# Two mixing stages whose engines each follow a planned order of small parts, with the merge's gates made inside them and kept in memory

## The reference, cut to what matters

```python
h = rms_norm_2(x, norm_mix[l])
z = h @ w_in[l]
c_q, c_kv, k_pe, hq, hf, hi, hg, g_a, g_b = jnp.split(z, offsets, axis=-1)
y_a = mla_mixer(c_q, c_kv, k_pe, ...) @ w_proj_a[l]
y_b = hgrn2_mixer(hq, hf, hi, hg, lower_bounds[l], ...) @ w_proj_b[l]
y = jax.nn.sigmoid(g_a) * y_a + jax.nn.sigmoid(g_b) * y_b
x = x + y @ w_out[l]
h = rms_norm_2(x, norm_ffn[l])
x = x + (jax.nn.silu(h @ w_gate[l]) * (h @ w_up[l])) @ w_down[l]
```

## Time and profile before

| | |
|---|---|
| median of 3 runs | 4867.03 us (4865.81 to 4867.9) |
| the profiled execution | 4877.7 us, of which the span of the page is 4876.4 |
| first block and what leads to layer 0's mixing | 2496.4 us |
| mixing stage, layer 0 / layer 1 | 616.7 / 616.3 us |
| merge and output product, layer 0 / layer 1 | 174.9 / 174.8 us |

### The profile page before, as it was taken

One profiled execution on the slowest core, in us unless ns is written; L12 is line 12 of the kernel. 1 busy time (PEld: TensorE's weight loads), 2 busy tenths in 40 slices (PEclk: granted clock), 3 DMA queues, 4 the chain that ended last, 5 costly groups with the idle time before them and its releaser, 6 DMA issues.

```text
span 4876.4 us, 51844 instructions
## 1 busy us (share of the span) xinstructions
PE 3921.2 (80%) x20620; PEld 3270.0 (67%) x20620; DVE 1520.6 (31%) x2463; ACT 1426.5 (29%) x2119; POOL 1356.5 (28%) x778
## 2 busy tenths in 40 slices
PE   7778888878889859999956555799998655588999
PEld 6767777777777757777655434587887543467887
DVE  2445455455440221111132533221102253313110
ACT  1322333433432200000033433333323433333331
POOL 1323334333324311101031211243442111134443
PEclk9888889989889958889977656899998766689999
DMA  4222201110103248879720100132332100022332
GB/s 135 70 57 57 57 27 31 31 27 22 31 22 104 59 117 277 270 248 291 252 80 26 31 9 13 35 100 81 96 95 55 39 21 2 13 57 82 92 98 87
DMA packets 467349, 401.74 MB, mean 82 GB/s; under 512 B 17910, under 2 KB 427043, under 8 KB 466981
## 3 DMA queue, kind: packets, MB, share of 16 engines
q1 hardware_dynamic: 456117, 361.70, 25.0%
q0 software_dynamic: 9520, 30.97, 1.9%
q10 hardware_dynamic: 1472, 5.77, 0.3%
HBM read 381.86 MB, written 16.53 MB: 82 GB/s over the span
## 4 chain that ended last, share of the span: by engine, by line
PE 71%; DVE 12%; ACT 9%; POOL 4%; issue 2%; DMA 1%; SPq 0%; DVEq 0%; ACTq 0%; POOLq 0%
PE bank L233 30%; PE bank L237 12%; PE bank L239 12%; PE bank L238 12%; ACT AR L134 5%; DVE AR L107 5%; POOL AR L107 3%; ACT L134 3%; DVE AR L118 2%; DVE AR L112 2%; PE bank L243 2%; PE bank L900 1%; DVE AR L126 1%; PE bank L1879 1%; POOL HTl L107 0%
## 5 line engine op out<-in xcount | busy, mean ns | idle before, releaser
L233 PE MATMUL bank<-AR 128*128 128x128 f32 (+5 forms) x5712 | 983.3, 332 | 412.8 <-POOL AR L107 247.5
L107 POOL TENSOR_TENSOR ring_r<-ring,high_r 128x1024 fp32r<-128x1024 f32 (+1 forms) x345 | 820.9, 2379 | 1424.4 <-ACT high_r L134 1416.4
L233 PEld LDWEIGHTS bank<-AR 128*128 128x128 f32 (+3 forms) x5712 | 847.2, 226 | 531.3 <-issue 270.7
L134 ACT ACTIVATE AR<-bank 128x512 f32<-128x512 f32 (+6 forms) x803 | 398.4, 496 | 1990.8 <-PE bank L233 1053.8
L107 DVE TENSOR_TENSOR AR<-AR,bank 128x512 f32<-128x512 f32 (+1 forms) x411 | 263.8, 642 | 1458.2 <-PE bank L239 766.9
L237 PE MATMUL bank<-HTh,high_r 128*128 128x512 f32 (+1 forms) x1608 | 658.7, 410 | 29.7 <-DVE HTl L107 13.3
L238 PE MATMUL bank<-HTl,high_r 128*128 128x512 f32 (+1 forms) x1608 | 640.6, 398 | 0.0
L239 PE MATMUL bank<-HTh,ring_r 128*128 128x512 f32 (+1 forms) x1608 | 640.1, 398 | 0.0
L134 ACT ACTIVATE high_r<-ring 128x1024 fp32r<-128x1024 f32 (+1 forms) x345 | 363.7, 1054 | 262.6 <-DMA ring<-in_w_down 141.9
L107 POOL TENSOR_TENSOR AR<-AR 128x512 f32<-128x512 f32 x112 | 167.0, 1491 | 822.2 <-ACT AR L134 817.7
L237 PEld LDWEIGHTS bank<-HTh,high_r 128*128 128x128 f32 (+1 forms) x1608 | 312.8, 195 | 97.3 <-DVE HTl L107 13.8
(11 more groups left out here) (146 smaller groups left out, 4877.6 us busy)
## 6 DMA issues: line engine op xcount, KB each, us to landing
ring<-in_w_in SPq DMA_DIRECT2D x154, 512.0 KB, 4.1
ring<-in_expert_w SPq DMA_DIRECT2D x61, 1024.0 KB, 11.2
high<-in_expert_w SPq DMA_DIRECT2D x60, 1024.0 KB, 11.8
ring<-in_ada_w SPq DMA_DIRECT2D x48, 512.0 KB, 4.0
ring<-in_w_gate SPq DMA_DIRECT2D x44, 512.0 KB, 3.8
ring<-in_w_up SPq DMA_DIRECT2D x44, 512.0 KB, 3.8
ring<-in_w_down SPq DMA_DIRECT2D x44, 512.0 KB, 3.6
AR<-in_expert_w SPq DMA_DIRECT2D x20, 1024.0 KB, 12.0
```

Source lines behind the costliest of these rows:

```text
L107: self.did(self.e.tensor_tensor(out, a, b, op), inc)
L134: self.did(self.e.activation(out, a, func, **kw), inc)
L233: m = pe.matmul(outap, l, r, start=(i == 0), stop=(i == n - 1))
```

## The change

The two hand-written lists, their interleaving and the banks of each are gone. In their place the stage is described as parts: each has one engine, a time in us by hand, the parts that it needs, and the bank that it opens or closes. A dense product of eight steps is eight parts.

`plan` simulates the five engines with these numbers. Each free engine takes, of its ready parts, the one with the longest way still behind it. Only PE has a second source: when none of its small parts is ready, it takes the next step of the dense products, which stand in one list in a fixed order. All eight banks are shared. What comes out is an order of its own for each engine, which `pe_mix`, `act_mix`, `vec_mix` and `pool_mix` then issue. The plan is made when the program is built; on the chip every queue is still in order.

```diff
+    HOP = 0.3
+    def plan(parts, fifo, nbank, spare, keep):
...
+            far[k] = parts[k][1] + HOP + max((far[n] for n in then[k]), default=0.0)
...
+                k = max((k for k in ready[e] if fits(k, keep.get(k[0], 0))), key=lambda k: far[k], default=None)
+                if k is not None:
+                    ready[e].remove(k)
+                elif e == "P" and head < len(fifo) and not left[fifo[head]] and fits(fifo[head], spare):
+                    k, head = fifo[head], head + 1
...
+    def mix_parts():
...
+            if what[-1] != "R":
+                part(("hi", i), "A", 1.05, ("load", i), *([("hi", hi[0])] if hi[0] is not None else []))
+                part(("lo", i), "G", 2.45, ("hi", i), *([("lo", hi[0])] if hi[0] is not None else []))
...
+        def gates(ns):
+            for i in ns:
+                dense(("G", i), 8, 0.69, [tile_of("in", 0, 1024, 2720 + i * 128, 128, "G")], opens=("G", i))
+                part(("Ga", i), "A", 1.7, ("G", i, 7), *([("Gs", i - 2)] if i > 1 else []))
+                part(("Gv", i), "V", 0.7, ("Ga", i), closes=("G", i))
+                part(("Gx", i), "A", 0.8, ("Gv", i))
+                part(("Gs", i), "S", 5.0, ("Gx", i))
...
+                for n in range(NT):
+                    part(("rn", wi, n), "V" if wi == 0 else "G", (1.9, 4.4)[wi], ("qi", wi))
+                    part(("rp", wi, n), "V" if wi == 0 else "G", (1.8, 3.0)[wi], ("rn", wi, n))
...
+        latent("cq", 0, 384, 384)
+        projection("f", 0)
+        latent("ck", 384, 256, 288)
+        projection("q", 0)
+        values(0)
+        projection("g", 0)
+        attention_in()
+        for h in range(1, 4):
+            projection("f", h)
+            projection("q", h)
+            if h == 2:
+                values(h)
+            projection("g", h)
+            gates(range(4 * h - 4, 4 * h))
+        gates(range(12, 16))
+        attention()
+        recurrence()
```

```diff
+            elif x in ("ga", "f1", "Ga"):
...
+                A.act(dst, mix_bk(g, i)[:, :], ACT.Abs)
+                A.act(dst, dst, ACT.Exp, scale=-1.0)
+                A.act(dst, dst, ACT.Ln, bias=1.0, inc=aEv)
+            elif x == "Gx":
...
+                A.act(stg[i % 2], stg[i % 2], ACT.Exp, inc=aEv)
+                see(A, "Gx", i)
+                gst[i % 2].then_inc(ac.dma_start(gate_d(i), stg[i % 2]), 16)
...
-            elif k == "g":
-                A.act(ybT[:, p[0]], b[:, :], ACT.Silu, inc=aEv)
```

```diff
+    def act_branch(l, its, MTp):
+        for q in range(2):
+            gst[q].upto(A, gst[q].n)
+        for j in range(16):
+            if j < 4:
+                act_gate(j)
...
+            act_split(it["t"] + HEAD)
+            if j + 4 < 16:
...
+                act_gate(j + 4)
...
+    def act_gate(i):
+        gld[i % 4].then_inc(ac.dma_start(tn2[:, i % 4], gate_d(i)), 16)
...
         sp_load(mg[0]["t"] - 1)
+        act_split(t0 + 1)
         act_squares(xn2, x_ready)
         act_norm(NT, 0, HT, tmpm)
-        act_split(its[0]["t"] + 2)
         vec_rows(xn2)
         vec_norm(NT, 0, HT, tmpm, lambda k: cb(f"mix{l}", k), None)
+        pool_split(t0 + 1)
         pool_norm(NT, 0, HT, tmpm)
-        pool_split(its[0]["t"] + 2)
```

More of the change, by code:

```diff
@@ new lines, in build, with mix_tiles @@
+    pt, fifo, mix_spec = mix_parts()
+    mix_order, mix_bank, mix_before, mix_last, mix_when = plan(pt, fifo, 8, 3, {"QK": 2, "Q": 2})
+    mix_at, mix_n = {}, {}
+    for e, o in mix_order.items():
+        mix_n[e] = 0
+        for k in o:
+            if k in mix_tile and (*k[:-1], k[-1] + 1) in mix_tile:
+                continue
+            if k[0] not in ("load", "hi", "lo", "Gs"):
+                mix_at[k[:-1] if k in mix_tile else k] = (e, mix_n[e])
+                mix_n[e] += 1
+    def mix_tiles(l):
+        src = {"in": d["w_in_2"][l], "uq": d["mla_w_uq_2"][l], "ukv": d["mla_w_ukv_2"][l]}
+        L_ = {"t0": len(tiles), "P": count["group"], "A": count["act"], "V": count["vec"], "old": dict(user)}
+        end = {}
+        for k in mix_order["P"]:
+            if k in mix_tile:
+                end[mix_tile[k]] = max(end.get(mix_tile[k], 0), mix_at[k[:-1]][1])
+        for i, (w, r0, r1, c0, n, how) in enumerate(mix_spec):
+            t = tile(src[w][r0:r1, c0:c0 + n], (r1 - r0) // 128, n, how)
+            tiles[t]["free"] = count["group"] + end[i] + 1
+        for e, n in (("P", "group"), ("A", "act"), ("V", "vec")):
+            count[n] += mix_n[e]
+        for b in range(8):
+            e, i = mix_at[mix_last[b]]
+            user[b] = {"ev": "act" if e == "A" else "vec", "e": L_[e] + i}
+        return L_
@@ new lines, in build, with see @@
+    gEv = sig("mix_part_pool")
+    gst = [sig(f"gate_stored{i}") for i in range(2)]
+    gld = [sig(f"gate_load{i}") for i in range(4)]
+    stg = [flat(cm[:, 2 + 4 * i:6 + 4 * i, :]) for i in range(2)]
+    gate_d = lambda i: y_d[i * 64:(i + 1) * 64, :].rearrange("r (a n) -> (r a) n", n=SEQ)
+    Lc = [None]
+    def see(q, *k):
+        e, i = mix_at[k]
+        if e == "G":
+            gEv.wait_ge(q, i + 1)
+        else:
+            {"P": pD, "A": aEv, "V": vEv}[e].upto(q, Lc[0][e] + i + 1)
@@ new lines, in pe_mix @@
+                    see(P, "le", h, 6)
+                    for j in range(NT):
+                        see(P, "va", h - h % 2, j)
+                see(P, "cv", h, n - 1) if n else see(P, "cz", h)
+                pD.then_inc(mm(tl(mix_bk("out", h), n), [(Sh, tl(qe, n)), (vtoken(h, n), AT[:, n])]))
+            elif x == "cu":
+                h, n = p
+                mix_free(*k)
+                see(P, "Tka", h)
+                for j in range(NT):
+                    see(P, "va", h - h % 2, j)
+                pD.then_inc(mm(mix_bk(*k)[:, 0:128], [(kdt[:, n], vtoken(h, n))]))
+            elif x == "op":
+                mix_free(*k)
+                see(P, "oa", p[0])
+                pD.then_inc(mm(mix_bk(*k)[:, :], [(ones, f1)]))
@@ L2402, in pe_ffn @@
     def pe_ffn(its):
         for it in its:
-            pe_proj(it)
+            w = pe_weight(it["t"])
+            bank_free(P, it)
+            for q in range(8):
+                m = mm3(bk[it["b"]][:, :], w[:, q, :], HT[:, q, :], q == 0, q == 7)
+            pD.then_inc(m)
     def act_ffn(its, end):
@@ L2430, in layer @@
         L_ = layers[l]
-        (its, at), mg, ow, ff, dn = L_["mix"], L_["merge"], L_["out"], L_["ffn"], L_["down"]
+        mg, ow, ff, dn = L_["merge"], L_["out"], L_["ffn"], L_["down"]
+        Lc[0] = L_["mix"]
+        t0 = Lc[0]["t0"]
         end = dn[-1]["t"] if l else last_tile_of_all
@@ L2445, in layer @@
         nV.wait_ge(P, 8)
-        pe_mix(its, at)
-        act_mix(its, at, end)
-        vec_mix(its, at, l)
-        pool_mix(its, at, end)
+        pe_mix()
+        act_mix(l)
+        vec_mix(l)
+        pool_mix(l)
         stage()
```

987 lines of the change are left out of this document (554 added, 433 removed).

## The result

The changed kernel takes 4426.8 us (median of 4 runs, 4407.5 to 4433.5) against 4866.4 before (4 runs): a ratio of 0.910, with an interval from 0.906 to 0.914. Predicted were 4320, with a range from 4220 to 4460. The profiled executions took 4433.5 and 4877.7.

A forecast was written before the change was run, and what follows sets the result against it. Hand-overs between engines bound the mixing stage, PE alone the merge. Per layer, 191.5 us saved in the stage and 81.4 in merge and joint, twice, plus 3.1 at layer 0's start: 548.9 saved, so 4320 us, range 4220 to 4460.

The forecast's parts named there:

- likeliest case: Whole kernel: mixing stage of 425 us, time 4320 us, own range 4240 to 4420, chance 0.70.
- rival 1: Mixing stage: in-order queues keep the hand-over's toll, late parts hold all behind; stage 500, time 4468 us, chance 0.15.
- signs of being wrong: Attention nearer 90 or 150 than 120 us, PE waiting over 20 in A or B, or for VectorE held by GpSimd.
- B: Mixing stage from first turned head of q to first logits: three engines near full together, 60 us.
- A: Mixing stage up to the first turned head of q: 138 us, including 3 for PE's slow clock at start.
- C: Attention stretch of the mixing stage, with head 2 between: 120 us, bounds 88 and 150.
- D: Mixing stage behind the attention, eleven gates and head 3: ScalarE, not PE, sets the end, 107 us.
- The joint: Between mixing stage and merge: PE waits for high and low parts of the attention output, 6 us lost.
- Merge: Merge with output product: the 16 gate products go, 87.4 us remain of 174.9, gate loads covered.
- Rival 2: ScalarE in the mixing stage: every table load costs double; stage 477, time 4422 us, chance 0.02.
- Rivals 3 and 4: Mixing stage: 3, plan holds, stage 370, 4208 us, chance 0.10; 4, waits stay, gates on top, 704, 4876, 0.03.
- rival 5: Merge: the gates' way through memory fails to hide; 5 us a layer, up to 20; no chance of its own.

The follow-up runs named there:

- one table: Changed kernel, but ScalarE loads one table set holding both Exp and Ln and keeps it; layers 536.3 and 533.7 us, against 576.9 and 573.8.
- experiment 3: Changed kernel, replanned with the planner tracking the held table and adding 1.28 us per load; stage 454.6 and 452.2 us, layers 564.2 and 561.2.

## Why the prediction was right, and which of its terms were not

**The sign and the kind** were right: PE's waits for scaled q, 123.8 us before, are 18.4 in the same view of the changed kernel's stage, and its transposes' wait for the probabilities, 83.3, is 7.5:

```profile
PE bank L243 <- DVE AR L107: 21.9, 4, 12.5
...
PE bank L233 <- POOL AR L107: 18.4, 9, 3.7
...
PE bank L243 <- DVE AR L112: 7.5, 7, 2.8
```

**The size** was too good by 58.5 us in layer 0 and 55.4 in layer 1, and the time by 107. It lies beyond the likeliest case's own range, 4240 to 4420, between it and rival 1 (a stage of 500, 4468). It is inside the range over all cases, but two of the prediction's own signs of being wrong came: the stage is over 450, and PE waits in B for more than 20 us (28.2). Nothing in the prediction separated what the order and the gates bring; the order, with what came along with it, brings all of it.

**B, 94 for 60: the step that failed.** "Three engines are near full together: 60" took the means of before and no latency. Two things showed. The table loads are 14 of the 34. For the other 20 the longest piece is head 1's chain: PE waits 12.5 us (11.3 with one table) for VectorE's pair of products, in the view above the longest part of "PE bank L243 <- DVE AR L107", 21.9. In this chain VectorE is slow beside GpSimd. Here are four scans before the change with GpSimd idle (head 0), then those of head 1 in the changed kernel's B, with a weight split that starts 0.41 us behind them, and the products that PE waits for, with k's norm on GpSimd beside them:

```profile
2561.30 1.80 DVE L2346 TENSOR_TENSOR_SCAN AR<-cm,AR 128x128 f32<-128x128 f32 x4
```

```profile
2645.22 3.94 DVE L2539 TENSOR_TENSOR_SCAN AR<-cm,AR 128x128 f32<-128x128 f32 x4
...
2651.25 4.13 DVE L107 TENSOR_TENSOR AR<-AR 128x512 f32<-128x512 f32 x3 [0.90 <-ACT AR L134]
```

```profile
2645.63 2.34 POOL L107 TENSOR_TENSOR ring_r<-ring,high_r 128x1024 fp32r<-128x1024 f32 x1 [5.82 <-ACT high_r L134]
2650.43 3.67 POOL L107 TENSOR_TENSOR AR<-AR 128x768 f32<-128x768 f32 x2 [2.46 <-DVE AR L122]
```

```profile
2654.79 1.09 PE L243 MATMUL bank<-cm,AR 128*128 128x128 f32 x4 [12.53 <-DVE AR L107]
```

The scans lost 3.94 - 1.80 = 2.14 us to a split of 2.34, and the three products about 2.1 (each takes 0.69 by itself). (The Trainium skill, "GPSIMD Engine Reference", Specifications, says that GpSimd and VectorE get in each other's way where VectorE reads two inputs from SBUF, as a scan here does; this trace agrees.) That is some 4 of the 12.5 us; in the rest the chain goes back and forth between ScalarE and VectorE. The prediction saw this, gave it 5 us each in A and C, and none in B. The mean over the stage is 0.96 us for 0.42 before a scan, and 0.89 for 0.75 a product of 512 columns. Measured prices in the plan took back 8 us of the stage. How the 20 us of B divide between VectorE's slowness and plain latency stays open: no run takes GpSimd's weight splits away from VectorE.

**A, 147 for 138.** My 3 us for the clock at the start were in place; the second fall, at the narrow matmuls, was missed. Wide ones give 8.4 and 8.2 us back.

**C, 115 for 120, and D, 112 for 107** were near, in part by luck. C was a choice between bounds, leaning on windows with a clock of 0.65 to 0.83; it ran at 0.90. In D the mechanism was only half right: ScalarE is busy 88.1 of 112.3, 78% and not over 90%, since it waited for PE until gate 11 and is behind PE only from gate 12 on. PE, with 94.3 for the 85 of the sum, is the busier of the two.

**The joint, 16 for 6.** The sum began at PE's last gate step and forgot that gate's own chain. Timelines of the changed kernel: ScalarE from gate 15 on, VectorE's low parts, PE's first branch product.

```profile
2958.86 0.60 ACT L134 ACTIVATE cm<-bank 128x512 f32<-128x512 f32 x1 [0.46 <-ACT cm L134]
...
2962.14 1.28 ACT L134 ACT_TABLE_LOAD   x1
2963.43 0.63 ACT L134 ACTIVATE cm<-cm 128x512 f32<-128x512 f32 x1
...
2964.47 3.35 ACT L134 ACTIVATE high_r<-ring 128x1024 fp32r<-128x1024 f32 x3 [0.40 <-ACT cm L134]
2967.85 5.26 ACT L134 ACTIVATE AR_r<-AR 128x512 fp32r<-128x512 f32 x8
```

```profile
2968.51 8.62 DVE L107 TENSOR_TENSOR AR_r<-AR,AR_r 128x512 fp32r<-128x512 f32 x4 [5.72 <-ACT AR_r L134]
```

```profile
2971.14 0.77 PE L237 MATMUL bank<-AR_r,high_r 128*128 128x512 f32 x1 [16.03 <-DVE AR_r L107]
```

PE stopped at 2955.1, ScalarE finished the gate at 2964.1: 9 us that I hadn't counted. Then 3.4 for the weights, and VectorE's first low part takes 2.2 us beside GpSimd, not 0.69. A gate comes every 5.7 us on ScalarE (gate 15 begins at 2958.86, gate 14 at 2953.20) where the prediction had 5.1, and so it is slower than PE's 5.46 and falls behind, gate by gate.

**Merge, 93.5 for 87.4.** PE is busy 92.3 of it: it begins at 1.2 GHz after the joint and waits 1 us for the second low part. The 87.4 were 1.1 too small as well: they are half of the 174.9 that ended 2.2 us early. The gates' loads were covered, as predicted; they landed 3.3 us after issue (median of 32), not 7.8.

**The rivals.** Rival 2, with a stage of 477, is nearer to the 467 measured than my 425, but for another reason. The drain of 1380 ns of the Trainium skill ("ScalarE: Activation LUTs", What ACT_TABLE_LOAD costs) would have given a stage of 483, and no trace here shows it. In the changed kernel too the next activation starts 0.01 us behind a load (2962.14 + 1.28, then 2963.43), and taking 60 loads out shortened the stage by less than their bare 77 us. Rival 1 came in part: its reason, a planner that leaves out the table loads, is worth 12 us a stage (experiment 3). Rivals 3 and 4 did not come, and rival 5, the gates' way through memory, cost nothing that the merge's windows show.

## What to carry to other kernels

Before work is moved into an engine's idle time, try the new order without it: here the order took away 169 of a stage's 238 us of idle time, and the work moved in filled only 4 of the 69 that were left, 12 once the table loads were gone. A planner needs the whole price of a part, with what its engine does between parts (table loads) and what a neighbour costs it, or its orders will be ahead of the truth just where several engines meet. Where a stage ends on one engine's queue, count from the last item's own chain, and look at which bank, buffer or slot the next stage asks for first.

## What the runs showed of the hardware that I had not expected

The granted clock fell from 1.00 to 0.50 while PE had no idle time, in a run of 96 matmuls of 32 columns; with 128 columns the same 96 kept it at 1.00 and took 10.6 us for 17.1 (A 8 us shorter in all). A busy share of 100% in the windows is no proof that the clock holds. And four VectorE scans of 1.80 us together lost 2.14 us to one GpSimd operation of 2.34 us beside them: nearly all of its length, not a share of it.
